# Moving the leftover strips of gate and up behind both weight pairs in a mixture-of-experts stage

## The reference, cut to what matters

```python
def swiglu(h, w_gu, w_down):
    g, u = jnp.split(h @ w_gu, 2, axis=-1)
    return (jax.nn.silu(g) * u) @ w_down
# moe_swiglu: logits = xt @ w_router; top 2 experts of each token; rows are collected by expert,
# each expert's rows go through swiglu with its own w_gu (1024 x 7168) and w_down (3584 x 1024),
# and every token adds its two results, weighted by the softmax of its two logits
```

## Time and profile before

| | us |
|---|---|
| median of 3 runs | 2503.71 (2499.23 to 2504.51) |
| profiled execution, its time | 2502.86 |
| its span | 2501.2 |
| PE busy | 2373.3 (95% of the span) |
| DVE, ACT, POOL busy | 1599.1, 1213.6, 204.4 |
| the 8 units in the span | about 1270 to 2405 |

### The profile page before, as it was taken

How to read it: one execution, slowest core, us unless ns; L and a number is a source line. 1 busy time by engine, 2 the same in 40 slices (tenths; PEclk the granted TensorE clock), 3 DMA queues, 4 the chain that set the end, 5 groups by cost and what they waited for, 6 DMA issues and landing times.

```text
span 2501.2 us, 35301 instructions
## 1 busy us (share of the span) xinstructions
PE 2373.3 (95%) x14626; PEld 1811.2 (72%) x14626; DVE 1599.1 (64%) x1807; ACT 1213.6 (49%) x1252; POOL 204.4 (8%) x214
## 2 busy tenths in 40 slices
PE   7999998999999999769979999999999999999977
PEld 4555555588888886768767788777887778777856
DVE  7997776323232334694366688667876688667864
ACT  3645343221222223654245577556765577556753
POOL 4007533000000000000000000001000000000010
PEclk9999998999999999889979999999999999999988
DMA  7668220433332232534177799779987799778960
GB/s 196 195 207 243 84 68 26 148 105 100 101 101 93 101 101 90 175 128 160 43 253 272 280 383 376 276 271 322 394 318 277 270 382 391 257 274 310 394 241 34
DMA packets 259806, 527.94 MB, mean 211 GB/s; under 512 B 19526, under 2 KB 61098, under 8 KB 256986
## 3 DMA queue, kind: packets, MB, share of 16 engines
q1 hardware_dynamic: 230250, 481.30, 54.4%
q0 software_dynamic: 6208, 25.78, 3.4%
q10 hardware_dynamic: 23184, 18.55, 2.3%
HBM read 496.03 MB, written 45.81 MB: 217 GB/s over the span
## 4 chain that ended last, share of the span: by engine, by line
PE 79%; DVE 11%; DMA 3%; ACT 3%; issue 2%; POOL 2%; ACTq 0%; POOLq 0%; DVEq 0%; SPq 0%
PE psum L1898 36%; PE psum L1424 17%; PE psum L1723 6%; PE psum L1961 4%; PE psum L1273 2%; PE psum L1994 2%; PE psum L1299 2%; PE psum L2053 2%; PE psum L1496 1%; PE psum L1938 1%; DVE stages L840 1%; DVE stages L850 1%; DVE stages L845 1%; DVE stages L841 1%; POOL stages L1091 1%
## 5 line engine op out<-in xcount | busy, mean ns | idle before, releaser
L1898 PE MATMUL psum<-stages_r 128*128 128x512 f32 x4032 | 951.7, 394 | 1.2 <-DVE stages_r L3500 0.6
L3500 DVE TENSOR_TENSOR stages_r<-kept,stages_r 128x2048 fp32r<-128x2048 f32 x336 | 769.6, 2291 | 270.3 <-ACT stages_r L2514 269.8
L1898 PEld LDWEIGHTS psum<-stages_r 128*128 128x128 f32 x4032 | 749.3, 188 | 173.8 <-issue 18.1
L2514 ACT ACTIVATE stages_r<-kept 128x2048 fp32r<-128x2048 f32 x336 | 643.7, 1916 | 374.5 <-PE psum L1898 319.5
L1424 PE MATMUL psum<-stages_r 128*128 128x512 f32 x1920 | 437.5, 390 | 3.2 <-ACT stages_r L2080 2.7
L1424 PEld LDWEIGHTS psum<-stages_r 128*128 128x128 f32 x1920 | 360.0, 188 | 79.4 <-ACT stages_r L2080 3.1
L3153 DVE TENSOR_TENSOR stages_r<-kept,stages_r 128x2048 fp32r<-128x2048 f32 x54 | 123.8, 2292 | 338.6 <-ACT stages_r L2372 338.6
L2372 ACT ACTIVATE stages_r<-kept 128x2048 fp32r<-128x2048 f32 x54 | 103.5, 1917 | 325.8 <-PE psum L1424 219.1
L1723 PE MATMUL psum<-stages_r,stages_front_r 128*128 128x512 f32 x672 | 152.6, 389 | 0.8 <-issue 0.8
L1723 PEld LDWEIGHTS psum<-stages_r,stages_front_r 128*128 128x128 f32 x672 | 126.1, 188 | 27.3 <-issue 1.2
L1299 PE MATMUL psum<-stages,kept 128*128 128x512 f32 x256 | 115.5, 598 | 0.0
(11 more groups left out here) (445 smaller groups left out, 2346.8 us busy)
## 6 DMA issues: line engine op xcount, KB each, us to landing
kept<-in_moe_w_gu_dram SPq DMA_DIRECT2D x224, 1024.0 KB, 7.9
kept<-in_moe_w_down_dram SPq DMA_DIRECT2D x112, 1024.0 KB, 8.4
kept<-in_ffn_w_gu_dram SPq DMA_DIRECT2D x28, 1024.0 KB, 5.1
kept<-in_ev_w_in_dram SPq DMA_DIRECT2D x16, 1024.0 KB, 8.0
kept<-in_ffn_w_down_dram SPq DMA_DIRECT2D x14, 1024.0 KB, 5.1
s_output_maps<-s_output_maps_by_state SPq DMA_DIRECT2D x32, 256.0 KB, 4.8
kept<-s_input_maps SPq DMA_DIRECT2D x8, 1024.0 KB, 4.9
kept<-s_output_maps SPq DMA_DIRECT2D x8, 1024.0 KB, 6.7
```

Of the source, the lines that this page charges most:

```text
L1898: m = pe.matmul(out_, a, b, start=start and n == 0, stop=stop and n == len(pairs) - 1, skip_group_check=True)
L2514: act.activation(w_high[n % WSLOTS], unit_tile(n), ACT.Copy).then_inc(s_wh, 1)
L3500: dve.tensor_tensor(w_low[n % WSLOTS], unit_tile(n), w_high[n % WSLOTS], ALU.subtract).then_inc(s_ws, 1)
```

## The change

In a large unit, the strips of the gate pair are issued behind the up pair, right before the strips of the up pair. ACT's silu of the leftover rows then waits for both groups of strips and stands behind all four splits of the step's pairs, and `hidden_high` and `hidden_low` of the step before stand where they do in a small unit. PE's wait for that silu ahead of the up strips is gone. The ring, its six slots and all other waits are as they were. Small units are unchanged.

```diff
@@ unit_pe, PE
                     rows_by(s_ % 2, gates)
+                    if s_:
+                        turn_hidden(s_ - 1)
+                    rows_by(up_bank(s_), ups)
                     if wide:
                         if s_:
                             pe.wait_ge(s_lhid, SSTEPS * (i // 2) + s_)
                         leftover_by(0, gates)
-                    if s_:
-                        turn_hidden(s_ - 1)
-                    rows_by(up_bank(s_), ups)
-                    if wide:
-                        pe.wait_ge(s_lsil, SSTEPS * (i // 2) + s_ + 1)
                         leftover_by(1, ups)
@@ unit_act, ACT
                 def leftover_silu(s_):
-                    act.wait_ge(s_lt, PER * (i // 2) + sgate_at(s_, 1) + 1)
+                    act.wait_ge(s_lt, PER * (i // 2) + sup_at(s_, 1) + 1)
...
                     act.activation(ssil[s_ % 2], psum[:, s_ % 2, :], ACT.Silu).then_inc(s_sil, 1)
-                    if wide:
-                        split(i, sgate_at(s_, 1) + WSLOTS)
-                        leftover_silu(s_)
                     if s_:
                         hidden_high(s_ - 1)
-                    if not wide:
-                        split(i, sgate_at(s_, 1) + WSLOTS)
+                    split(i, sgate_at(s_, 1) + WSLOTS)
                     split(i, sup_at(s_, 0) + WSLOTS)
                     split(i, sup_at(s_, 1) + WSLOTS)
+                    if wide:
+                        leftover_silu(s_)
@@ unit_dve, DVE
                     split(i, sgate_at(s_, 0) + WSLOTS)
-                    if s_ and not wide:
+                    if s_:
                         hidden_low(s_ - 1)
                     split(i, sgate_at(s_, 1) + WSLOTS)
-                    if s_ and wide:
-                        hidden_low(s_ - 1)
                     split(i, sup_at(s_, 0) + WSLOTS)
```

## The result

The changed kernel takes 2541.51 us in the median of 4 runs (2533.98 to 2544.47), the kernel before 2502.30. The ratio is 1.0156 (1.0133 to 1.0179): 1.6% slower. A second comparison on another chip gave 1.0168 (1.0152 to 1.0183). The direction was forecast; the time lies 0.5 us above the range and the loss of 39 us is well over the 23 forecast.

What follows compares the result with a forecast made beforehand. PE, busy nearly throughout, was taken to bound the kernel. Switches -7.9, gate tiles +2, turns +16.4 and +5.6, clock +6.8 summed to +22.9 on 2502.86 us: forecast 2526 us on the median, range 2511 to 2541.

Steps and rivals of the forecast that it cites:

- Cheaper switches: PE in large units: less switching between kinds of matmul saves 1.97 us a unit, 7.9 us in four.
- The turn of step 6: Fifth transpose on PE waits 4.1 us for `leftover_hidden`, held behind tile 40's split; four times, 16.4 us.
- of step 0: Turn of step 0, in step 1: PE waits 1.4 us behind late tile 6; four times, 5.6 us.
- The clock: Behind each 4.1 us stall PE runs 3.4 us at half clock, 1.7 us lost; four times, 6.8 us.
- The first gate tile: Steps 2 to 6: cover of 0.3 us before PE needs it; 0.1 us mean at 20 places, 2 us.
- the other tiles of the burst follow 2.5 us or so apart and are due 2.8 apart, so the first decides: Gate and up tiles in steps 2 to 6: only the burst's first tile can make PE wait; later ones add nothing.
- The sign that the prediction names for being wrong: PE waiting over 0.3 us at L1898, the split products, in most middle steps.
- The up tile itself, ready at L + 10.87, waits inside this: Step 1, L the joined strips' start: the up tile's lateness falls within the 1.4 us wait, adding nothing.
- the burst slows its first transfer: Rival, chance 0.07: DMA, each step's first gate tile; four transfers share engines, flight 6.8 us, total 2563 us.
- The rival with the long half clock: Rival, chance 0.10: the stalls come and each costs 10.2 us of half clock; 2539 us.
- The rival of the other side: Rival, chance 0.08: slots of tiles 34 and 0 have more slack, so only the switches count; 2495 us.

Runs made afterwards that it cites:

- Seven slots: A seventh raw-tile slot in the expert units, on the kernel before (2499.64 us, ratio 0.9998) and on the changed kernel (2492.76 us, ratio 0.9970).
- the two traces: Profiles of the changed kernel: its first measurement (median 2541.51 us, profiled execution 2533.98) and its repeat, unchanged, beside the seven-slot kernels (2540.09 us).
- the joined kernel with seven slots: The changed kernel with a seventh raw-tile slot, the last projection's weights loaded behind the units: 2492.76 us, ratio 0.9970 to before.
- the held-back experiment: Changed kernel with leftover silu and product ahead of the late split, next step's first up tile issued only after the second gate tile landed: 2562.09 us, ratio 1.0251.
- the paced one: Changed kernel with SP holding back up tiles (and tiles 8 and 9) so at most two burst transfers are under way: 2543.23 us, ratio 1.0165.
- the filled: Changed kernel with the four transposes in large units' step 6 issued ten times over, keeping PE at work through the long wait: 2534.78 us, ratio 1.0138.

## Why the prediction was wrong

- **Cheaper switches**, -7.9 us: right. Seven slots isolate them: stages of 1133.3 and 1124.3, so -9.0.
- **The turn of step 6 and of step 0**, +16.4 and +5.6: right in place, cause and size. 20.8 and 22.7 us lost in the two traces. The long waits had 3.5 to 4.1 us idle in the first trace and 3.6 to 4.9 in the second, the short ones 1.1 to 1.2.
- **The clock**, +6.8: right in sum, 7.3 and 7.4, and in part by luck. In the first trace it was half for 6.8 us behind two stops, 3.4 behind one and not at all behind the fourth, where I had 3.4 behind each; in the second for 6.8 behind one and 3.4 behind three.
- **The first gate tile**, +2: this is the step that failed, at "the other tiles of the burst follow 2.5 us or so apart and are due 2.8 apart, so the first decides". The term was 2 us, with a bound of 6; the waits for split tiles cost 13.6 and 16.1. The first tile landed late in two places only, both in unit 2 (1.9 us). The second tile lands 3.9 us behind the first in the median of the 20 places, and 2.65 before. In 12 places it was 3.6 to 4.1 us behind, and these are the 12 where PE stopped for it (8.4 us); in the other eight it was 2.7 to 3.3. With 1.1 us too much and about 0.4 of cover, 0.6 are waited. The sign that the prediction names for being wrong, over 0.3 us at L1898 in most middle steps, came true: at the two gate tiles 13 of the 20 have it. "The up tile itself, ready at L + 10.87, waits inside this" left out the second up tile: that put at nothing what cost 1.9 us in three of the four units.
- **Idle time taken for lost time.** The prediction has a stop cost what PE waits. Each of the 16 stops between the first and the second tile of a pair cost 0.16 us more than its idle time at the stop, and 0.13 to 0.17 us more in the 12 products behind it.
- The four terms of the changed kernel's first ledger, 20.8 + 13.6 + 7.3 - 9.0, less the 0.9 lost before, are 31.8 of the 35.0 us. For the other 3.2 I set its PE instructions one by one beside those of the joined kernel with seven slots, which has the same ones in the same order and no such stop. Its stage is 46.1 us longer than that one's: 35.3 at stops, 6.9 in the stretches at half clock, 3.3 in the 30 instructions behind each stop, and 0.6 elsewhere. So most of what the ledger leaves open is what the stops do to the products behind them.
- Of the rivals, "the burst slows its first transfer" was at the right resource and the wrong transfer: the first took 4.8 to 5.7 us in all but two of 28 places. The rival with the long half clock gave 2539, next to what was measured, but by chance: the clock cost 7.3 us and not the 20.4 that it had. The rival of the other side gave 2495, which is what the seventh slot brought about.

**Why the second tile is late.** The traces show which share of it is late, and the held-back experiment that nothing queued behind it is needed for that. A transfer lands in 16 shares. In the burst at 1666.00 (flight of its first and second transfer):

```profile
DMA to landing us min/median/max: 5.1/5.1/5.1
...
DMA to landing us min/median/max: 8.3/8.3/8.3
```

fifteen shares of the second were there 6.9 us after its issue and the last one at 8.3. From 1666.0 to 1674.5, the queues have:

```profile
q1 hardware_dynamic: 1320, 2.64, 89.3%
q8 instruction: 1, 0.02, 0.8%
```

One 16 KB transfer of instructions (q8), which starts 4.5 us into the burst and takes 1.0 us. I compared its start with the flight in all 20 places. Changed kernel: in the 12 places where it starts 2.8 to 6.3 us into the burst the second tile flies 8.1 to 8.4 us; in the other 8, where it starts within 1.3 us of the burst's start, 7.1 to 8.1. Before: 8.2 in the two where it starts 2.6 and 3.6 us in, 6.9 to 7.1 in the 6 places where it starts 7.0 us in or later, 6.9 to 7.9 in the other 12, within 1.1 us of the start. The first tile fits in: it flies over 6 us in five of these 40 places, and in these five, and in no other, such a transfer starts 1.1 to 3.6 us into the burst (6.2 to 6.5 us of flight); two of them are the stops at the first gate tile in unit 2. The units have about as many instruction transfers as before (70 against 69); what changed is where in the burst they fall. In the held-back kernel it is 7.9 to 8.5 us in the 12 places with such a start and 7.0 to 8.0 in the other 8. This points to a share that is held up by the instruction transfer, but it is a coincidence in time: I tried no kernel that moves the transfer. That the 128 strips in a row, PE's densest run of instructions, draw it in is argued, not shown.

## What to carry to other kernels

When a group of small operations is moved behind a larger one to save switches, ask first which buffer its inputs hold and how many are in the ring; a move of 6 us that saves 9 us over a stage cost 39 with six slots and gained 7 with seven. Then read the written order of the other engines at each place where the late buffer is due: an operation that needs no new data should not stand behind one that does. And price a burst by its second and later transfers too, each stop of PE at its idle time plus about 0.3 us.

## What the runs showed of the hardware

- A 1 MB transfer with nothing ahead of it landed in 4.8 to 5.7 us in 26 of 28 places of the changed kernel, mostly 5.1 to 5.3. The second of a burst landed 2.65 us behind the first in the median of the kernel before, and 3.9 in the changed one, where in 12 of 20 bursts an instruction transfer started 2.8 to 6.3 us in.
- PE's clock fell to half behind 11 of 12 stops of 3.5 to 4.9 us (both traces of the changed kernel, and the paced one), and behind 4 of 25 stops of 1.4 to 2.2 us: one each in the filled and the paced kernel (1.89 and 1.88 us), two in the held one (1.99 and 2.04 us, not behind one of 2.19). No stop of 1.0 to 1.3 us was followed by it.
- A stop of PE between 512-column products cost 0.16 us more than the profile's idle time, and 0.13 to 0.17 us more in the 12 products behind it, in each of 16 places. Over the 28 stops of the ledger the first part is 4.4 us (34.4 lost, 30.0 idle).
